# A diffusion backbone step on one core: normalisation moved through the router and pooling products, pooling as banded products, expert results combined by token, modulation chunks spread over the program

## The chip, the cores and the metric

One of the eight cores of a Trainium2 chip runs the whole step, in float32. The metric is the device time of one execution in microseconds (us). PE is TensorE, DVE VectorE, ACT ScalarE, POOL GpSimd, SP SyncE, which only issues transfers here.

## What is computed

128 context tokens and 256 latent tokens of width 1024 go through two layers. Every sublayer reads `rms_norm(x, g) * (1 + scale) + shift`, and its result is added to x times a gate; shift, scale and gate come from a conditioning vector, one for the context and one for the latents. Cut to what matters:

```python
for l in range(2):
    sh1, sc1, g1, sh2, sc2, g2 = split(silu(cond) @ ada_w[l] + ada_b[l])   # ada_w[l]: 1024 x 6144
    h = rms_norm(x, norm_mix_g[l]) * (1 + sc1) + sh1
    m = attention(h) if l == 0 else multi_scale_pool(h, pool_w, pool_scale)
    x = x + g1 * m
    h = rms_norm(x, norm_ffn_g[l]) * (1 + sc2) + sh2
    x = x + g2 * moe(h)        # router h @ (1024 x 36): best of 4 groups, best 2 of its 8 experts
# multi_scale_pool: four groups of 256 features; mean over a centred window of 2, 4, 8, 16 tokens
# minus the token itself, then a 256 x 256 product per group
# moe: 32 experts a layer, each gate and up 1024 x 256 and down 256 x 1024, weighted sum of two
```

## The kernel before

The program is written out engine by engine, with a counting semaphore for each kind of result; the order on each engine is the order of its code. Its stages, one after the other:

- **Opening.** The six vectors of a layer are a product of 1024 x 6144, cut in 12 chunks of 512 columns, numbered 0 to 23 over both layers. A chunk is a load of 2 MB (`load_ada`), eight products on PE (`ada`, L1185), a copy by ACT (`ada_copy`) and four small products that turn the result into columns (`ada_vectors`, L1195). Chunks 0 to 3 are needed before the first product with the attention weights. A load waits for `ada_mm` of the chunk that held its place.
- **QKV products**, nine groups (L1254), with chunks 4 to 11 between them.
- **Attention**, 24 units (16 of the latents with 384 keys, 8 of the context with 128), two heads each. A unit u has its scores on PE (L1297), their maximum on DVE (L913), the exponential on ACT (L670), the reciprocal of the sum on DVE (L920), the scaling by it on POOL (L494, two instructions), transposes on PE (L1325, L1332) and a copy by DVE (L928). In every fourth step PE multiplies with the values (L1314). Chunks 12 to 17 stand in steps 0, 1, 2, 3, 4 and 7. From step 19 on come the output products of the latents (L1360, eight), after the last step those of the context (L1368, eight).
- **Normalisation and router.** `norm_pe`, `norm_act`, `norm_dve` and `modulate_act` form sums of squares by a product with ones (L1375), the root and reciprocal over 128 x 384, and h in feature-major form (hT); the router logits are a product of hT (L1389), turned once more (L1393). `rows_by_token` turns hT into rows by token (L1406), ACT copies them out (L743), and they are written to DRAM; meanwhile `router` on DVE picks the experts. PE counts them (L1415), DVE gives each token its slot in a table of tiles of 64 rows, and POOL gathers the rows.
- **Experts**, 32 tiles a layer and those beyond 64 rows behind them (`extra_tiles`). The weights lie in a ring of four places and a fifth place in `adaw`. SP loads tile s when the tile that held its place has been used: `load_tile` waits for `gu_mm` and `down_mm`. Three transfers make a tile: gate and up 1 MB each, down 1 MB. Results are scattered to DRAM by POOL.
- **Between the layers.** The results are read back (`yrow`) and combined by products with diagonal matrices (L1582); x is normalised, `pool_group` forms window sums on DVE and POOL, and PE multiplies them with the pooling weights (L1599). Then norm, router and experts of layer 1, and the end, where DVE and ACT combine the results by token.

## Time and profile before

| | us |
|---|---|
| runs, median of 3 (lowest to highest) | 945.75 (945.08 to 947.68) |
| the profiled execution, whole | 946.34 |
| its span, first to last instruction | 944.5 |
| PE busy | 759.0 |
| DVE, ACT, POOL busy | 265.7, 188.4, 250.7 |
| moved by the transfers | 294.94 MB, 312 GB/s over the span |
| mean granted clock of TensorE | 0.923 |

Busy time is a mean over stages; what ends last in each stage is read from the chain of waits, the timeline and the windows by stage.

### The profile page before, as it was taken

How to read it: one execution, taken by the hardware profiler on the slowest of the kernel's cores; microseconds unless marked ns; L12 is line 12 of the kernel's file. 1: busy time of each engine (PE TensorE's matmuls, PEld its weight loads, DVE VectorE, ACT ScalarE, POOL GpSimd, SP SyncE). 2: the span in 40 equal slices, each digit the busy share in tenths (PEclk: the TensorE clock that was granted, in tenths of full speed). 3: DMA queues.
4: the chain of work that ended last, by engine and by line, in shares of the span. 5: the costliest groups of instructions: out<-in, count | busy, mean ns of one | idle time of the engine just before them, and what ended most of it. 6: DMA issues, size and time to landing. Idle time of an engine off the chain costs nothing.

```text
span 944.5 us, 12930 instructions
## 1 busy us (share of the span) xinstructions
PE 759.0 (80%) x4601; PEld 408.2 (43%) x4601; DVE 265.7 (28%) x632; ACT 188.4 (20%) x413; POOL 250.7 (27%) x347
## 2 busy tenths in 40 slices
PE   2899989889986999878877867277899978877850
PEld 1534444448833554434433436134555444443420
DVE  0403424532165111111111103976311111111105
ACT  3111144631152011001111102235111101101101
POOL 0000406752002333333232211600243323332212
PEclk9799999989997999999999998677899999999985
DMA  9999779400896999999999959323299999999933
GB/s 325 386 389 370 220 210 387 159 2 1 316 345 234 404 412 411 415 413 413 414 411 413 393 220 396 142 86 133 105 399 407 411 415 416 414 415 413 402 117 155
DMA packets 81126, 294.94 MB, mean 312 GB/s; under 512 B 11624, under 2 KB 12064, under 8 KB 64448
## 3 DMA queue, kind: packets, MB, share of 16 engines
q1 hardware_dynamic: 68064, 273.84, 73.9%
q0 software_dynamic: 11296, 15.09, 4.9%
q10 hardware_dynamic: 1728, 5.51, 1.5%
q8 instruction: 24, 0.39, 0.2%
q14 instruction: 14, 0.11, 0.0%
HBM read 293.84 MB, written 22.02 MB: 334 GB/s over the span
## 4 chain that ended last, share of the span: by engine, by line
PE 50%; DMA 33%; DVE 7%; ACT 3%; issue 3%; SPq 2%; POOL 1%; ACTq 0%; POOLq 0%; DVEq 0%
DMA ring<-in_moe_w_up 25%; PE bank L1492 13%; PE bank L1254 7%; PE bank L1516 6%; PE bank L1185 3%; PE bank L1360 3%; DMA ring<-in_moe_w_down 2%; PE bank L1468 2%; PE bank L1375 2%; PE bank L1195 2%; PE bank L1314 2%; PE bank L1368 2%; PE bank L1389 1%; PE bank L1582 1%; DMA adaw<-in_ada_w 1%
## 5 line engine op out<-in xcount | busy, mean ns | idle before, releaser
L1492 PE MATMUL bank<-ring,qkv 128*64 128x256 f32 x2016 | 247.5, 401 | 64.8 <-DMA ring<-in_moe_w_up 55.6
L1492 PEld LDWEIGHTS bank<-ring,qkv 128*64 128x64 f32 x2016 | 149.4, 144 | 145.2 <-DMA ring<-in_moe_w_up 45.5
L530 POOL DMA_INDIRECT results<-adaw,scur x65 | 66.3, 1020 | 295.5 <-ACT adaw L777 263.2
L1084 DVE COPY qkv<-bank 128x512 f32<-128x512 f32 x64 | 44.2, 691 | 326.5 <-PE bank L1468 298.6
L1516 PE MATMUL bank<-ring,qkv 128*64 128x512 f32 x504 | 122.0, 604 | 1.2 <-DVE qkv L1096 0.8
L520 POOL DMA_INDIRECT adaw<-rows,gcur x65 | 67.9, 1045 | 50.6 <-POOL gcur L517 41.2
L771 ACT ACTIVATE qkv<-bank 128x128 f32<-128x128 f32 x64 | 17.7, 277 | 305.9 <-PE bank L1492 259.6
L1254 PE MATMUL bank<-ring,hT 128*128 128x512 f32 x144 | 65.4, 609 | 1.2 <-DVE hT L855 1.2
L494 POOL TENSOR_SCALAR ring<-ring,rt 128x384 f32<-128x384 f32 (+1 forms) x48 | 49.6, 1047 | 63.2 <-DVE rt L920 63.1
L777 ACT ACTIVATE adaw<-bank 128x512 f32<-128x512 f32 x64 | 38.2, 597 | 140.0 <-PE bank L1516 140.0
L1516 PEld LDWEIGHTS bank<-ring,qkv 128*64 128x64 f32 x504 | 31.0, 136 | 47.5 <-issue 45.6
L1468 PE MATMUL bank<-con,adaw 128*128 128x128 f32 x260 | 43.0, 288 | 6.1 <-DMA adaw<-rows,gcur 5.2
L1254 PEld LDWEIGHTS bank<-ring,hT 128*128 128x128 f32 x144 | 27.3, 194 | 33.9 <-issue 32.6
L1468 PEld LDWEIGHTS bank<-con,adaw 128*128 128x128 f32 x260 | 27.6, 141 | 32.2 <-issue 32.2
L1096 DVE COPY qkv<-bank 128x128 f32<-128x128 f32 x64 | 18.7, 291 | 75.7 <-PE bank L1501 75.7
L1501 PEld LDWEIGHTS bank<-con,qkv 128*128 128x128 f32 x64 | 9.0, 141 | 52.8 <-DVE qkv L1090 49.9
L1185 PE MATMUL bank<-adaw,condT 128*32 128x512 f32 x256 | 30.8, 598 | 1.1 <-DMA adaw<-in_ada_w 1.0
L670 ACT ACTIVATE ring<-bank,ss 128x384 f32<-128x384 f32 (+1 forms) x48 | 24.0, 505 | 37.7 <-DVE ss L913 37.5
L1599 PE MATMUL bank<-hT,xtok 128*128 128x384 f32 x32 | 15.9, 670 | 18.4 <-POOL hT L293 13.3
L1360 PE MATMUL bank<-hT,ring 128*128 128x256 f32 x128 | 29.1, 380 | 0.0
L483 POOL DMA_DIRECT2D ring<-in_cache_k x1 | 0.5, 537 | 105.7 <-PE bank L1254 105.7
L1195 PEld LDWEIGHTS bank<-con,adas 128*128 128x128 f32 x176 | 21.1, 191 | 15.9 <-issue 15.8
(217 smaller groups left out, 783.0 us busy)
## 6 DMA issues: line engine op xcount, KB each, us to landing
ring<-in_moe_w_gate SPq DMA_DIRECT2D x63, 1024.0 KB
ring<-in_moe_w_up SPq DMA_DIRECT2D x63, 1024.0 KB
ring<-in_moe_w_down SPq DMA_DIRECT2D x63, 1024.0 KB
adaw<-in_ada_w SPq DMA_DIRECT2D x16, 2048.0 KB, 12.6
ring<-in_ada_w SPq DMA_DIRECT2D x8, 2048.0 KB, 12.9
ring<-in_attn_w_qkv SPq DMA_DIRECT2D x3, 2048.0 KB, 19.6
adaw<-results SPq DMA_DIRECT2D x12, 512.0 KB, 6.3
ring<-in_attn_w_o SPq DMA_DIRECT2D x1, 4096.0 KB, 19.5
```

The source lines that it names most:

```text
L494: last = G.tensor_scalar(probs[:, u % 4, j, 0:nk], probs[:, u % 4, j, 0:nk], rt[:, 64 + 2 * (u % 4) + j:65 + 2 * (u % 4) + j], None, ALU.mult)
L520: pool.indirect_dma_start(xg[:, b], None, rows, bass.IndirectOffsetOnAxis(ap=gcur[:, b:b + 1], axis=0), bounds_check=row_limit, oob_is_err ...
L530: pool.indirect_dma_start(res, bass.IndirectOffsetOnAxis(ap=scur[:, b:b + 1], axis=0), yout[:, b], None, bounds_check=res_limit, oob_is_er ...
L777: A.activation(yout[:, q], bank[4 + q % 2][:, :], ACT.Copy).then_inc(y_ready, 1)
L1084: V.tensor_copy(xgT[:, p], bank[2][:, :]).then_inc(xgT_ready, 1)
L1185: last = T.matmul(out[32 * j:32 * j + 32, :], condT[:, k, :], ada_place[(i + 2) % 3][:, k, :], start=half == 0, stop=half == 1, skip_group ...
L1195: last = T.matmul(bank[2][:, at:at + 2], adas[:, i % 4, j * P:(j + 1) * P], C("sel2"), start=True, stop=True)
L1254: last = T.matmul(bank[5 + g % 3][:, :], hT[:, k, t * P:(t + 1) * P], wqkv[n][:, k, :], start=k == 0, stop=k == KD - 1)
L1360: last = T.matmul(bank[WO_BANKS[d % 2]][:, 0:NTOK - CTX], wo[:, k, d * P:(d + 1) * P], hT[:, k, CTX:NTOK], start=k == 0, stop=k == KD - 1)
L1468: last = T.transpose(bank[2][:, i * P:(i + 1) * P], xg[:, q, i * P:(i + 1) * P], ident)
L1492: last = T.matmul(bank[p][64 * a:64 * a + 64, 0:2 * P], xk[:, k % 4, k // 4], w[:, :, k, a * P:(a + 1) * P], start=k == 0, stop=k == KD - ...
L1516: last = T.matmul(bank[4 + p][64 * a:64 * a + 64, :], hidT[:, p, 64 * j:64 * j + 64], w[j][:, a * 512:(a + 1) * 512], start=j == 0, stop=j ...
```

## The change

Nothing but the form changes; the same numbers are computed. It has these parts.

1. **Layouts.** The weights of ada_w, QKV, the output product and the experts are laid out ahead of the launch so that each partition reads one run: 16 KB for a chunk (eight runs of 2 KB before), one transfer of 16 KB per partition for gate and up (two of 8 KB before), one of 8 KB for down (two runs of 4 KB before).
2. **Opening.** x and the constants are loaded first; the small vectors go through ACT's queue; chunk 0 stands behind the transposes of x.
3. **Chunks spread.** Chunks 4 to 9 are between the QKV groups, none in attention, 10 to 15 around the router of layer 0, 16 to 21 between the layers, 22 and 23 beside the router of layer 1.
4. **Attention.** The scaling of the probabilities goes from POOL to DVE.
5. **Router.** The logits are products of the plain x (xT) with router weights that were multiplied by the scale (`router_weights`); the sums of squares are products with one column of ones; the reciprocal root enters the logits as one number per token, and the shift's part is added (`logit_shift`). The rows by token are x times the scale, turned, times the root on ACT, and POOL adds a row of the shift (`shift_rows_mm`, `token_rows_mm`).
6. **Between the layers.** The two results of a token are combined by ACT and DVE (`y_first`, `y_both`) and then turned; pooling is a product with scaled weights (L1738), times the root, plus a product of the shift, and then a product with a banded matrix of 128 x 128 with two corners of 8 columns (L1775).

The core of the diff:

```diff
-        AFTER_QKV = {g: 3 + g for g in range(1, 9)}
-        FIRST_SIDE = AFTER_QKV[8] + 1
-        LATE = 2 * NCH - 6
-        SIDE = {step: ("ada", FIRST_SIDE + i) for i, step in enumerate((0, 1, 2, 3, 4, 7))}
+        AFTER_QKV = {g: 3 + g for g in range(1, 7)}
+        LATE = AFTER_QKV[6] + 1
+        BETWEEN = LATE + 6
+        SIDE = {7: ("q", 0), 8: ("q", 1), 11: ("k", 0)}
...
-                for i, w in enumerate((moe_w_gate, moe_w_up)):
-                    sp.dma_start(ring[:, b, i * KD * FE:(i + 1) * KD * FE],
-                                 w[l, bass.ds(e, 1)].rearrange("o (p k) f -> (o p) (k f)", k=KD)).then_inc(arrived, 16)
+                sp.dma_start(ring[:, b, 0:2 * KD * FE],
+                             moe_w_in[l, bass.ds(e, 1)].rearrange("o p n -> (o p) n")).then_inc(arrived, 16)
...
+                if l == 0:
+                    load_ada(BETWEEN)
+                    sp.wait_ge(down_mm, LAST[0] + 1)
+                    load_ada(BETWEEN + 1)
                 sp.wait_ge(x_down[l], 1)
                 n_extra = sp.value_load(extra_e[0:1, EXTRA:EXTRA + 1], min_val=0, max_val=EXTRA)
                 with sp.If(n_extra > 0):
                     load_extra(0)
-                if l == 0:
-                    sp.wait_ge(down_mm, LAST[0] + 1)
-                    load_expert(1, 0)
...
-                for j in range(2):
-                    last = G.tensor_scalar(probs[:, u % 4, j, 0:nk], probs[:, u % 4, j, 0:nk],
-                                           rt[:, 64 + 2 * (u % 4) + j:65 + 2 * (u % 4) + j], None, ALU.mult)
+                    order(V.reciprocal(rt[:, 64 + 2 * (v % 4):66 + 2 * (v % 4)], rt[:, 2 * v:2 * v + 2]))
+                    for j in range(2):
+                        c = 64 + 2 * (v % 4) + j
+                        last = V.tensor_scalar(probs[:, v % 4, j, 0:nk], probs[:, v % 4, j, 0:nk], rt[:, c:c + 1], None,
+                                               ALU.mult)
...
+                for i, t in enumerate(ROW_TILES):
+                    pool.wait_ge(hb_copied, l * 10 + (4, 6, 10)[i])
+                    G.tensor_tensor(xtok[:, t, :], xtok[:, t, :], shift_rows[int(t > 0)], ALU.add).then_inc(rows_ready, 1)
...
+                    pool.wait_ge(shw_mm, 4)
+                    pool.wait_ge(wp_ctx, 1)
+                    by_row = poolw.rearrange("p g k n -> p (g k) n")
+                    G.tensor_tensor(by_row, by_row, mods[:, 1, KD:2 * KD, 1:2].to_broadcast([P, KD, 2 * P]), ALU.mult)\
+                        .then_inc(wp_lat, 1)
...
+            y_both(0)
+            y_both(1)
+            add_experts(0)
+            y_both(2)
+            add_experts(1)
+            pooled_rows(0)
+            add_experts(2)
+            pooled_rows(1)
+            pooled_rows(2)
+            dve.wait_ge(ada_vec, BETWEEN + 6)
+            modulation(1, 2, 5)
...
+                if l == 1:
+                    act.wait_ge(s_rowsout, 48 + 16 * TT)
+                    for n in range(6):
+                        act.wait_ge(x1_mm, n + 1)
```

Where the change moves instructions, first SP's queue at the end of layer 0's experts. Before, the rows from the last load of the tiles on (`L458`, `L451` and `L459` read and test the number of further tiles):

```order
L372 DMA ring<-in_moe_w_down 128x2x1024
L458 TENSOR_LOAD extra_e
L458 ISA x2
L459 COMPARE_AND_BRANCH
L451 TENSOR_LOAD extra_e
L451 ISA x2
L368 ISA
L368 DMA ring<-in_moe_w_gate 128x2048
L368 DMA ring<-in_moe_w_up 128x2048
L372 DMA ring<-in_moe_w_down 128x2x1024
```

and now, from the same place:

```order
L364 DMA ring<-in_moe_w_out 128x2048
L357 DMA adaw<-in_ada_w 128x4096
L357 DMA ring<-in_ada_w 128x4096
L449 TENSOR_LOAD extra_e
L449 ISA x2
L450 COMPARE_AND_BRANCH
L438 TENSOR_LOAD extra_e
L438 ISA x2
L360 ISA
L360 DMA ring<-in_moe_w_in 128x4096
L364 ISA
L364 DMA ring<-in_moe_w_out 128x2048
```

Chunks 16 and 17 stand ahead of the weights of the further tile.

The second place is PE at the router of layer 0. Before, from the logits to the counting of the experts (L1415):

```order
L1389 MATMUL bank<-hT,wr 36x384 x8
L1393 MATMUL bank<-con,rt 128x36 x3
L1195 MATMUL bank<-con,adas 128x2 x4
L1185 MATMUL bank<-adaw,condT 32x512 x8
L1195 MATMUL bank<-con,adas 128x2 x4
L1406 MATMUL bank<-con,hT 128x128 x24
L1415 MATMUL bank<-rt,con 128x32 x6
```

and now, from the last logits (L1450) to the counting (L1533), with the row of the shift (L1500), the rows by token (L1507) and the chunks (L1273, L1283):

```order
L1450 MATMUL bank<-qkv,xT 128x36
L1500 MATMUL bank<-con,mods 128x128 x8
L1507 MATMUL bank<-con,hT 128x128 x16
L1273 MATMUL bank<-ring,condT 32x512 x8
L1500 MATMUL bank<-con,mods 128x128 x8
L1507 MATMUL bank<-con,hT 128x128 x8
L1273 MATMUL bank<-adaw,condT 32x512 x8
L1283 MATMUL bank<-con,adas 128x2 x4
L1533 MATMUL bank<-rt,con 128x32 x6
L1536 MATMUL bank<-con,rt 32x1 x3
L1273 MATMUL bank<-adaw,condT 32x512 x8
L1283 MATMUL bank<-con,adas 128x2 x4
```

Sixteen products of the shift and a second chunk stand ahead of the counting, and a third chunk behind it.

The third is PE between the layers, where one block of products with diagonals (L1582) stood ahead of the norm. Now, with the product of the shift (L1705), the turning of the combined rows (L1716), the sums of squares (L1445), the pooling product (L1738) and a chunk after each:

```order
L1273 MATMUL bank<-adaw,condT 32x512 x8
L1705 MATMUL bank<-xtok,mods 128x256 x16
L1716 MATMUL bank<-con,adaw 128x128 x8
L1273 MATMUL bank<-ring,condT 32x512 x8
L1283 MATMUL bank<-con,adas 128x2 x4
L1716 MATMUL bank<-con,adaw 128x128 x8
L1445 MATMUL bank<-con,qkv 128x1 x8
L1738 MATMUL bank<-hT,xT 128x256 x8
L1273 MATMUL bank<-ring,condT 32x512 x8
L1283 MATMUL bank<-con,adas 128x2 x4
L1716 MATMUL bank<-con,adaw 128x128 x8
```

The two token tiles that follow repeat this, and two more chunks come ahead of the banded products (L1775).

## Rows read from the trace of the kernel before

**Rows 1.** Windows by stage: us, busy time and count by engine, granted clock, transfers.

```profile
44.00:136.50 92.50, 89.96 (x360) 40.22 (x360) 28.65 (x47) 20.05 (x42) 9.86 (x12) 0.98 0.87 296
136.50:207.50 71.00, 61.45 (x384) 30.96 (x384) 33.57 (x68) 35.26 (x110) 42.50 (x36) 0.95 0.57 210
...
241.00:273.40 32.40, 30.04 (x197) 19.03 (x195) 12.37 (x28) 12.25 (x21) 0.00 (x0) 1.00 0.95 367
273.40:304.40 31.00, 22.22 (x163) 13.23 (x162) 18.15 (x81) 11.02 (x14) 4.59 (x6) 0.84 0.70 256
304.40:554.80 250.40, 213.43 (x1440) 109.97 (x1441) 38.55 (x97) 27.97 (x64) 78.80 (x127) 0.96 1.01 405
554.80:643.30 88.50, 54.15 (x221) 31.30 (x222) 50.59 (x93) 21.32 (x38) 21.77 (x16) 0.81 0.44 178
643.30:672.20 28.90, 21.82 (x99) 15.33 (x98) 19.02 (x76) 12.09 (x16) 3.23 (x6) 0.70 0.34 114
672.20:913.70 241.50, 209.46 (x1436) 108.08 (x1436) 37.14 (x95) 27.97 (x64) 74.35 (x123) 0.97 0.94 378
```

**Rows 2.** The page's 40 slices of 23.6 us: transfers in GB/s.

```profile
GB/s 325 386 389 370 220 210 387 159 2 1 316 345 234 404 412 411 415 413 413 414 411 413 393 220 396 142 86 133 105 399 407 411 415 416 414 415 413 402 117 155
```

**Rows 3.** The chain of waits, opening and QKV: start us, us, what.

```profile
16.54 3.23 ACT qkv L611 x6
...
59.82 1.85 PE bank L1185 x16
...
70.60 0.98 PE bank L1195 x8
...
134.64 1.88 PE bank L1195 x16
```

**Rows 4.** The chain of waits in attention and its output products.

```profile
142.20 12.51 DMA adaw<-in_ada_w
...
161.28 2.80 PE bank L1314 x12
...
175.79 2.79 PE bank L1314 x12
...
188.55 2.80 PE bank L1314 x12
...
241.05 14.29 PE bank L1368 x128
```

**Rows 5.** The timeline of DVE and POOL: scaling forms, an attention unit.

```profile
26.19 2.08 DVE L829 TENSOR_SCALAR xtok<-xtok,ss 128x1024 f32<-128x1024 f32 x3 [4.70 <-PE bank L1207]
...
174.60 0.69 DVE L928 COPY ring<-bank 128x512 f32<-128x512 f32 x1 [0.43 <-PE bank L1325]
...
175.67 0.96 DVE L913 TENSOR_REDUCE ss<-bank 128x2 f32<-128x768 f32 x1 [0.38 <-PE bank L1297]
...
181.40 4.90 POOL L494 TENSOR_SCALAR ring<-ring,rt 128x384 f32<-128x384 f32 x4 [2.15 <-DVE rt L920]
```

**Rows 6.** The timeline at the router of layer 0.

```profile
277.77 1.93 ACT L743 ACTIVATE xtok<-bank 128x512 f32<-128x512 f32 x2 [0.85 <-PE bank L1406]
...
282.57 1.42 PE L1415 MATMUL bank<-rt,con 128*128 128x32 f32 x12
```

**Rows 7.** The chain of waits around the end of layer 0's experts.

```profile
535.00 19.69 DMA ring<-in_moe_w_down
...
566.47 4.15 DMA adaw<-results
```

**Rows 8.** The timeline at the end: POOL and DVE, adjacent and at once.

```profile
928.85 1.22 DVE L1160 TENSOR_TENSOR adaw<-adaw,hT 128x1024 f32<-128x1024 f32 x1
...
930.15 3.31 POOL L596 TENSOR_TENSOR xtok<-adaw,xtok 128x1024 f32<-128x1024 f32 x1 [2.42 <-DVE adaw L1160]
931.30 3.25 DVE L1160 TENSOR_TENSOR adaw<-adaw,hT 128x1024 f32<-128x1024 f32 x1
```

**Rows 9.** The chain of waits at the router of layer 1.

```profile
650.53 6.45 DMA rows<-xtok
```

More of the change, by code:

```diff
@@ L1439, in _ @@
                 if l == 0:
-                    for i in range(LATE + 3, 2 * NCH - 1):
+                    for i in range(LATE + 3, BETWEEN - 1):
                         ada(i)
@@ new lines, in _, with feature_sums @@
+                    ada_vectors(BETWEEN + 3)
+                    ada(BETWEEN + 5)
+                    ada_vectors(BETWEEN + 4)
+                    ada_vectors(BETWEEN + 5)
+                    pe.wait_ge(ada_copied, BETWEEN + 6)
+                    def feature_sums(k):
+                        for t in range(TT):
+                            last = stat(2 * KD + 6 + k + 1, 0, sq[:, k % 2, t * P:(t + 1) * P], t, k == 0 and t == 0, k == KD - 1)
+                        last.then_inc(st_mm, 1)
@@ new lines, in _ @@
+                    for n in range(KD):
+                        pe.wait_ge(z_ready, 5 if n < 3 else 6)
+                        if n >= 4:
+                            pe.wait_ge(x_new[2], 2 * (n - 4) + 2)
+                        out, cols = bank[BAND_BANKS[n % 4]], slice(n * P, (n + 1) * P)
+                        parts = ((0, 0, 0, P), (1, P, P, P), (2, 2 * P, 2 * P, P), (1, 2 * P, 3 * P, 8), (2, 2 * P - 8, 3 * P + 8, 8))
+                        for i, (t, a, b, w) in enumerate(parts):
+                            last = T.matmul(out[:, a:a + w], z[:, t, cols], bands[:, n // 2, b:b + w], start=i == 0, stop=True,
+                                            skip_group_check=True)
+                        last.then_inc(mix_mm[2], 1)
+                        if n:
+                            feature_sums(n - 1)
+                        if n == 3:
+                            pe.wait_ge(mods_ready, 4)
+                            logit_shift(1, bank[1])
+                        if n >= 4:
+                            logits(n - 4, range(TT))
```

760 lines of the change are left out of this document (436 added, 324 removed).

## The prediction

> **What bounds it now.** I read the windows by stage first [rows 1]: two expert stages of 250.4 and 241.5 us, and six shorter stages ahead of, between and behind them. In the expert stages the transfers are busy for 1.01 and 0.94 of the time at 405 and 378 GB/s, and the slices of the page stay at 411 to 416 GB/s [rows 2]: the ring of weights sets the pace. It can't run ahead by more than five tiles, so an expert stage begins when the router releases it and lasts as long as its bytes; what comes ahead shifts it one for one. In the other stages the chain of waits runs over PE, with DVE and ACT hops. Two things stand out. In attention the chain waits 12.51 us for a chunk's load [rows 4], while the slices behind it show 159, 2 and 1 GB/s [rows 2]: loads are too late for one place and absent in the next. Between the layers (554.8 to 672.2) transfers are busy for 0.44 and 0.34 of the time and PE for 54.15 of 88.5 us [rows 1]: there is room for chunks, in bytes and partly on PE.
>
> **The change, stage by stage**, against the profiled execution (946.34, span 944.5, 1.8 around it).
>
> *Opening.* ACT's squares of x start at 16.54 [rows 3]. With x (1.57 MB) and the constants (0.59 MB) first, at 386 GB/s [rows 2] they need 5.6 us; with some 4 us for start, landing and the two small steps on the vectors ahead of them the squares start near 9.9, 6.7 earlier. Chunk 0 now stands behind the transposes: 1.85 + 0.98 = 2.83 us [rows 3]. Net -3.9.
>
> *QKV.* Two chunks leave. What leaves the chain is 1.85 after the eighth group, and behind the ninth 1.85 + 1.88 [rows 3], of which I keep 1.9 as the wait for the copies of q and k that these products covered: -3.7.
>
> *Attention.* It lasts 71.0 us from the first scores to the first output product [rows 1]. The wait of 12.51 and six chunks (17.0) leave, but the pace does not follow, since DVE takes over the scaling. A unit costs DVE 0.96 + 0.69 [rows 5], 0.2 for the reciprocal, and now two scalings of 384 elements. Three of 1024 elements take 2.08 [rows 5], 0.69 each; with a fixed part of 0.1 to 0.2 that is 0.3 to 0.4 for 384, taken as 0.35. Together 2.6 us a unit, against 1.2 for one POOL scaling [rows 5], 2.45 a unit. From one value product to the next, four units, it took 188.55 - 175.79 = 12.8 us under POOL [rows 4]; DVE has 10.4 of work in them and waits some 2 us behind the value product: 12.4. So the steady part gains almost nothing. The first six units took 161.28 - 136.5 = 24.8 us [rows 1, 4] with the wait and five chunks; DVE's work there is 6 x 2.6 plus the last norm of q and k and one modulation, 17.2. With 12.9, 12.4, 10.6 and 6.1 for the rest: 59.2, that is -11.8. The bounds are -2 (DVE as slow as POOL was) and -25 (all that leaves counts).
>
> *Latent output products*: untouched. *Context products and logits*: 32.4 before [rows 1]. Now 14.3 [rows 4] plus 64 small products at 0.245 (four in 0.98 [rows 3]), 15.7: 30.0, and 0.3 for the last hop. -2.1.
>
> *Router of layer 0.* DVE picks the experts in some thirty short operations, an estimated 7 us, but PE counts only 282.57 - 273.4 = 9.2 us after them, since the turned rows stand in front and each of the six banks waits for an ACT copy, 1.93 for two [rows 6]. Now ten banks and a chunk stand in front. ACT first copies hT of the context (2.4 us), then five pairs at 2.35 with the gap, and PE adds a second chunk, 2.83: the counting starts 15.2 after the logits, +6.0. The chunk behind the counting takes 2.83, where eight short DVE operations, an estimated 1.5, were waited for: +1.3. POOL's three additions (3.31 or less each, [rows 8]) are done in time for the gather. +7.4 with rounding.
>
> *Experts of layer 0*: 29 tiles, one of them the further one, whose weights were issued at 535.00 and landed 19.69 later [rows 7], right behind tile 31. Two chunks now stand between: 4.19 MB at 425 GB/s, +9.8. The longer runs are worth something: chunks and QKV weights in runs of 2 KB move at 386 to 389, experts in runs of 6 KB on average at 413 to 415 [rows 2]. A fixed 9 ns a run explains both; with 370, the slice behind, 14 ns. A tile has 512 runs before and 256 now, on 16 engines, so it gains 0.14 to 0.22 us; I take 0.2, since the gathers' short rows also slow the experts' slices: -5.8. Net +4.0. The Trainium skill ("DMA: Bandwidth & Descriptors", section "Why small descriptors are slow") speaks against this: it gives a fixed overhead of about 3 cycles a packet beside one per 32 bytes, and at 6 KB that is 1.5%, so that halving the count saves 0.8%, an estimated 0.06 us a tile. The rate of the short runs agrees with more than that.
>
> *Between the layers*, from the arrival of the last weights at 554.8 to the logits, 88.5 before [rows 1]. The results are back 15.8 us after it as before (566.47 + 4.15 [rows 7]). From there PE is the chain: per token tile, eight transposes, eight sums, eight products of 256 columns (1.3 + 2.0 + 3.5) and a chunk 2.83, with ACT's and DVE's combination 1.2 + 1.3 ahead of the first: 39 us from there to the last chunk, waits for ACT and DVE included (some 7); then eight groups of bands, sums and logits at 2.7 and the 16 shift products, 26.5. The logits come 83.8 after the weights: -4.7. POOL's scaling of the pooling weights, 128 x 2048 with two inputs, has twice the elements of the one of 3.31 [rows 8] and falls on the first combination on DVE. DVE's 1.22 became 3.25 beside POOL in [rows 8], so I add 3.0. Net -1.7. The loads fit: 3.1 MB of results, six chunks and five tiles, 31 MB, are 76 us of 120.
>
> *Router of layer 1.* 28.9 before. Ten banks and two chunks bring the counting to an estimated 15.6 after the logits. The x copies of ACT wait for the last write of rows (6.45 [rows 9]), which POOL's addition makes later: 21.8 instead of 13.7 (650.53 + 6.45 - 643.3). +8.1.
>
> *Experts of layer 1*: 27 tiles behind the first five gain 27 x 0.2: -5.4. The end, 30.8, stays.
>
> Sum: -3.9 - 3.7 - 11.8 - 2.1 + 7.4 + 4.0 - 1.7 + 8.1 - 5.4 = -9.1. 946.3 - 9.1 = 937.2; the median lies 0.6 below the profiled execution, so 936.6.
>
> **Rivals.** *A: the released time comes through.* The 12.51 wait and the chunks were the chain in attention, and the rows cost the routers less than I count, because ACT's pairs overlap. It speaks for it that PE is busy for 61 of 71 us there; against it, that POOL's four scalings of 4.90 stand in the chain's place once the chunks are past. -10 more in attention and -6 in the routers: 921. Chance 0.27.
>
> *B: long runs give nothing*, by the rule above or because a run is cut at 8 KB. The rows only show 2 KB against 6 KB. Then +11.2 on the experts: 948, no change. Chance 0.13.
>
> *C, slower: PE's clock between the layers.* The granted clock was 0.81 and 0.70 there [rows 1], after waits of PE for other engines. The new stage holds some 70 us of PE work in short products with hops over ACT and DVE. If a quarter of it runs at 1.2 GHz instead of 2.4, it doubles: +17, so 954. It decides from 6 us on (no gain) and 12 us on (slower). For it speaks that each token tile crosses PE, ACT and DVE three times; against it that the chunks fill PE's waits. Chance 0.17.
>
> Mine has 0.43, with a range of its own of 928 to 946.
>
> **Numbers.** Within 0.3% (942.9 to 948.6) no measurement of this kernel can tell a change. Faster: 0.36 of my 0.43, all of A, 0.02 of B, 0.03 of C, 0.68. Same: 0.06, 0, 0.08, 0.02, 0.16. Slower: 0.01, 0, 0.03, 0.12, 0.16. The range reaches past A's time and nearly to C's, 918 to 951, with about 0.1 left out on either side.
>
> **What would show it.** Squares near 10 and first QKV product near 40; value products of attention 12.4 apart, with DVE, not POOL, in the chain; counting of experts 15 us after the logits in both routers; transfers at 418 or more in full expert slices; the further tile's weights some 255 us after the first tile; DVE's first combination stretched beside POOL. The prediction is wrong where the value products come 10 us apart (A), the slices stay at 413 (B), or the clock falls below 0.8 between the layers (C).

## The result and the profile after

The changed kernel takes 988.81 us, median of 4 runs (983.29 to 989.41), beside 945.41 for the kernel before in the same comparison: a ratio of 1.0443, 95% interval 1.0413 to 1.0474. It is 4.4% slower; 936.6 was predicted, and no rival came near. The profiled execution took 988.32 with a span of 986.5, 42.0 more than before.

The page of the changed kernel, its 40 slices of 24.7 us (compare [rows 2]):

```profile
PEclk9999988998878999999999787757699999999985
...
GB/s 357 427 430 241 193 1 11 1 13 243 176 400 331 421 420 421 420 421 420 422 416 363 144 344 229 326 3 154 298 276 408 419 420 424 421 422 420 415 115 151
```

Most full slices now move 419 to 424 GB/s. The clock falls to 5, 7 and 6 tenths in slices 27 to 29 of the 40, at the end of the stage between the layers and in the router behind it; the transfers show 3 GB/s in slice 27.

The windows by stage answer to [rows 1]. The columns are those of [rows 1]; the stages end at the same events: first scores, first output product, the context's products, logits, first expert product, last weights, logits of layer 1, first expert product, last one.

```profile
42.60:131.10 88.50, 84.20 (x310) 37.57 (x311) 27.94 (x45) 17.70 (x38) 9.87 (x12) 0.98 0.74 274
131.10:189.90 58.80, 46.29 (x239) 23.47 (x240) 45.85 (x105) 32.80 (x105) 0.00 (x0) 0.88 0.02 5
189.90:223.40 33.50, 33.50 (x167) 26.59 (x166) 10.55 (x35) 6.84 (x25) 0.00 (x0) 1.00 0.08 24
223.40:256.90 33.50, 33.50 (x259) 33.50 (x258) 5.38 (x17) 5.03 (x18) 0.00 (x0) 0.85 0.43 173
256.90:299.80 42.90, 37.24 (x242) 21.76 (x241) 21.68 (x80) 18.54 (x28) 12.31 (x10) 0.76 0.82 332
299.80:556.50 256.70, 207.21 (x1442) 113.94 (x1443) 37.88 (x96) 28.00 (x64) 78.43 (x128) 0.97 0.98 403
556.50:670.40 113.90, 103.89 (x548) 83.67 (x549) 27.15 (x63) 23.02 (x43) 9.52 (x11) 0.71 0.49 195
670.40:716.30 45.90, 31.56 (x204) 25.31 (x204) 19.06 (x76) 19.08 (x26) 12.59 (x10) 0.72 0.61 244
716.30:954.00 237.70, 208.01 (x1436) 111.15 (x1436) 37.19 (x95) 28.70 (x65) 74.19 (x123) 0.98 0.93 384
```

Set against the stages before, with the prediction's terms. The window of [rows 1] that ends at 304.40 stops 0.8 us ahead of the first expert product, which came at 305.16; the table counts to the product in both kernels:

| stage | before | after | change | predicted |
|---|---|---|---|---|
| opening, to the first QKV product | 44.2 | 42.6 | -1.5 | -3.9 |
| QKV | 92.4 | 88.5 | -3.9 | -3.7 |
| attention | 71.0 | 58.8 | -12.2 | -11.8 |
| output products of the latents | 33.5 | 33.5 | 0 | 0 |
| context products and logits | 32.4 | 33.5 | +1.1 | -2.1 |
| router of layer 0 | 31.8 | 42.9 | +11.1 | +7.4 |
| experts of layer 0 | 249.7 | 256.6 | +7.0 | +4.0 |
| between the layers | 88.5 | 113.9 | +25.4 | -1.7 |
| router of layer 1 | 28.9 | 45.9 | +17.0 | +8.1 |
| experts of layer 1 | 241.5 | 237.7 | -3.8 | -5.4 |
| end | 30.8 | 32.5 | +1.7 | 0 |

Over half of the 51 us by which the prediction missed lie between the layers, and 9 in the router behind it. Look at PE there: it was busy for 54.15 of 88.5 us before [rows 1] and is busy for 103.89 of 113.9 now, so it hardly waits, and its clock is still at 0.71. Windows of the changed kernel at the places where the clock is low:

```profile
238.00:248.00 10.00, 10.00 (x49) 10.00 (x49) 0.61 (x2) 0.62 (x2) 0.00 (x0) 0.51 0.00 0
276.00:288.00 12.00, 12.00 (x60) 5.99 (x56) 7.01 (x27) 1.19 (x2) 0.00 (x0) 0.50 1.01 425
...
590.00:600.00 10.00, 9.70 (x35) 8.58 (x36) 5.30 (x16) 3.85 (x5) 0.00 (x0) 0.50 0.94 397
...
636.00:670.00 34.00, 34.00 (x162) 34.00 (x161) 3.89 (x11) 5.00 (x12) 3.02 (x5) 0.50 0.15 61
```

In the first and the last PE is busy for the whole window, and so is the loading of its weights (PEld, behind PE in a row, which in the expert stages is some half of PE's). It runs at 1.2 GHz for 34 us without having waited in them. What it does there, PE's groups by line and shape from 649 to 664:

```profile
L1450 PE MATMUL bank<-qkv,xT 128*128 128x36 f32 x23 | 5.7, 407 | 0.0
L1775 PE MATMUL bank<-qkv,adaw 128*128 128x128 f32 x18 | 4.9, 444 | 0.0
L1445 PE MATMUL bank<-con,qkv 128*128 128x1 f32 x20 | 4.8, 352 | 0.0
L1775 PE MATMUL bank<-qkv,adaw 128*128 128x8 f32 x12 | 2.6, 326 | 0.0
```

The new forms: sums of squares of one column (`L1445`), logits of 36 (`L1450`), the bands with their corners of 8 (`L1775`). The kernel before has these steps as products of 384 columns with ones (L1375) and with the logits' weights (L1389). More of the difference is seen in the chain of waits:

```profile
536.19 20.14 DMA ring<-in_moe_w_out
...
556.47 6.67 PE bank L1618 x32
...
576.26 1.15 ACT adaw L731
...
577.44 3.08 DVE adaw L1194
...
684.71 2.36 POOL xtok L492
687.06 0.02 issue
687.08 14.91 DMA rows<-xtok
```

The write of the rows takes 14.91 us instead of 6.45 [rows 9]. The timeline of SP and ACT's queue in the changed kernel shows what was issued around it (L360 and L364 are tiles of weights, L416 the fifth place, L726 the rows):

```profile
679.58 0.33 SPq L360 DMA_DIRECT2D ring<-in_moe_w_in  x1
...
685.21 0.33 SPq L360 DMA_DIRECT2D ring<-in_moe_w_in  x1
...
686.15 0.44 SPq L416 DMA_DIRECT2D adaw<-in_moe_w_in  x1
...
687.08 0.33 ACTq L726 DMA_DIRECT2D rows<-xtok  x1
```

Before 679.58 the transfers stood at 3 GB/s for a slice: the places of tiles 1 and 2 held chunks 22 and 23, which PE takes up only in the router. So these weights are issued right ahead of the rows.

### The profile page after: what moved, and what is told of

Read it like the earlier page. It is cut to its first block, busy times and chain, and to the rows that moved or that the text cites. A ratio compares the mean times of both kernels' runs of the same rounds, so it can differ in the third digit from the quotient of the medians.

```text
span 986.5 us, 13540 instructions
## 1 busy us (share of the span) xinstructions
PE 808.4 (82%) x4981; PEld 491.9 (50%) x4981; DVE 253.3 (26%) x635; ACT 195.1 (20%) x433; POOL 206.5 (21%) x302
## 4 chain that ended last, share of the span: by engine, by line
PE 58%; DMA 28%; DVE 5%; ACT 3%; issue 3%; POOL 1%; SPq 1%; ACTq 0%; POOLq 0%; DVEq 0%
DMA ring<-in_moe_w_in 21%; PE bank L1618 14%; PE bank L1642 7%; PE bank L1342 7%; PE bank L1273 5%; PE bank L1438 3%; PE bank L1594 2%; PE bank L1445 2%; DMA adaw<-rows,gcur 2%; DMA ring<-in_moe_w_out 2%; PE bank L1283 2%; PE bank L1481 2%; PE bank L1450 2%; PE bank L1738 2%; DMA rows<-xtok 2%
## 5 line engine op out<-in xcount | busy, mean ns | idle before, releaser
L1618 PE MATMUL bank<-ring,qkv 128*64 128x256 f32 x2016 | 242.8, 395 | 73.6 <-issue 41.3
L1618 PEld LDWEIGHTS bank<-ring,qkv 128*64 128x64 f32 x2016 | 157.7, 142 | 140.9 <-issue 79.4
L1642 PEld LDWEIGHTS bank<-ring,qkv 128*64 128x64 f32 x504 | 31.0, 136 | 47.5 <-issue 45.6
L492 POOL TENSOR_TENSOR xtok<-xtok,qkv 128x1024 f32<-128x1024 f32 x6 | 14.2, 2372 | 168.0 <-ACT xtok L718 168.0
L1627 PEld LDWEIGHTS bank<-con,qkv 128*128 128x128 f32 x64 | 9.0, 141 | 52.7 <-DVE qkv L1145 51.1
L1283 PEld LDWEIGHTS bank<-con,adas 128*128 128x128 f32 x192 | 24.9, 204 | 20.2 <-issue 19.6
L1273 PE MATMUL bank<-ring,condT 128*32 128x512 f32 x208 | 29.1, 684 | 0.0
L618 ACT ACTIVATE adas<-bank 128x512 f32<-128x512 f32 x24 | 14.3, 596 | 74.3 <-PE bank L1273 74.3
L1283 PE MATMUL bank<-con,adas 128*128 128x2 f32 x192 | 26.5, 262 | 0.6 <-ACT adas L618 0.6
## 6 DMA issues: line engine op xcount, KB each, us to landing
adaw<-in_ada_w SPq DMA_DIRECT2D x11, 2048.0 KB, 12.2
```

What stands on the lines that cost most here:

```text
L1273: last = T.matmul(out[32 * j:32 * j + 32, :], condT[:, k, :], w[:, k, :], start=half == 0, stop=half == 1, skip_group_check=True)
L1283: last = T.matmul(bank[2][:, at:at + 2], adas[:, i % 4, j * P:(j + 1) * P], C("sel2"), start=True, stop=True)
L1618: last = T.matmul(bank[p][64 * a:64 * a + 64, 0:2 * P], xk[:, k % 4, k // 4], w[:, :, k, a * P:(a + 1) * P], start=k == 0, stop=k == KD - ...
L1642: last = T.matmul(bank[4 + p][64 * a:64 * a + 64, :], hidT[:, p, 64 * j:64 * j + 64], w[j][:, a * 512:(a + 1) * 512], start=j == 0, stop=j ...
```

## The experiments

Each is told with its edit, what was on record before it ran, and what it gave. "Before" was measured beside each (medians of 945.1 to 946.3), and the ratios are to it. Times are medians of 4 to 10 runs.

**1. The sums over 128 columns.** The same sums, formed 128 times side by side; column 0 is read.

```diff
-                return T.matmul(bank[b][:, col:col + 1], src, ones[:, 0:1], start=first, stop=last, skip_group_check=True)
+                return T.matmul(bank[b][:, P * col:P * col + P], src, ones, start=first, stop=last, skip_group_check=True)
```

> The changed kernel, with the sums of squares as products with 128 columns of ones instead of one column (only column 0 is read); all else as it was. Theory narrow: PE's granted clock stays at 0.50 from 636 to 675 although PE is busy all the time, because products of one and 36 columns follow each other there; with 128 columns it returns to 1.00, a group of bands, sums and logits goes from 4.7 us to about 2.8, eight of them give -15, and the context products of layer 0 another -2 to -4: 970 to 974. Theory wait: the clock fell because PE waited for DVE at 631 to 632 and it would stay down whatever the columns are; then the wider products only cost more at the low clock, 24 of them at some 0.2 us, +3 to +8: 991 to 996.

Measured: 960.81 (958.0 to 962.05), ratio 1.0156 (1.0126 to 1.0186). More work on PE, and 28.0 us less, well beyond the 15 to 19 that theory narrow had. Its windows for the chunks and pooling products, the bands, and the router of layer 1:

```profile
562.50:622.50 60.00, 51.02 (x317) 36.65 (x316) 19.63 (x47) 15.34 (x26) 5.46 (x5) 0.89 0.78 306
622.50:644.00 21.50, 21.38 (x189) 21.27 (x190) 4.72 (x14) 7.16 (x18) 4.07 (x7) 1.00 0.43 180
644.00:689.50 45.50, 31.37 (x202) 25.12 (x201) 20.95 (x76) 18.97 (x26) 13.24 (x12) 0.74 0.62 248
```

The bands with their sums and logits, 189 records of PE in both kernels, take 21.5 us instead of 38.4 (632.0 to 670.4), at a clock of 1.00. The groups by shape among its bands, from 632 to 640:

```profile
L1445 PE MATMUL bank<-con,qkv 128*128 128x128 f32 x23 | 3.5, 286 | 0.0
L1450 PE MATMUL bank<-qkv,xT 128*128 128x36 f32 x22 | 2.8, 264 | 0.0
L1775 PE MATMUL bank<-qkv,adaw 128*128 128x128 f32 x18 | 2.7, 288 | 0.0
```

A sum of 128 columns takes 286 ns here, one of a single column 352 ns there. A group of bands, sums and logits goes from 4.7 us to 1.09 + 0.77 + 0.59 = 2.45. From the last weights to the logits of layer 1 it is 91.5 us (552.5 to 644.0) instead of 113.9: 16.9 less in the bands and 5.5 less ahead of them, where sums stand too. Another 3.4 us come in layer 0. Both kernels have a wait of PE of 0.81 us for ACT just ahead of the bands, so theory wait falls there.

**2. The logits over 128 columns, the sums left at one.** The products read on behind the 36 columns of the router weights into what follows them, and nobody reads the result of that.

```diff
-                    out = T.matmul(bank[6][:, 16 + 36 * t:52 + 36 * t], xT[:, k, t * P:(t + 1) * P], wrs[:, int(t > 0), k, :],
+                    a = 3392 + (int(t > 0) * KD + k) * (NG + NE)
+                    out = T.matmul(bank[6][:, P * t:P * t + P], xT[:, k, t * P:(t + 1) * P], free[:, a:a + P],
```

> The changed kernel, with the logit products of both routers run over 128 columns instead of 36 (the columns behind the 36 are not read) and the sums of squares left at one column. Theory columns: what holds the clock at 0.50 among the bands is that few columns pass in the time that the weight loads take, whichever product they belong to; 92 more columns in 24 products a layer are some two thirds of what the wide sums added (127 in 24), so the clock rises here too and most of the 28 us come back: 962 to 975. Theory sums: it is the products of a single column that lower it; the logits only begin at the fifth band, so at most the later half gains: 978 to 990.

Measured: 975.06 (972.95 to 984.43), ratio 1.0299 (1.0253 to 1.0344): 14 us less. The windows of this kernel:

```profile
648.00:652.00 4.00, 4.00 (x20) 4.00 (x20) 0.33 (x1) 1.04 (x3) 0.60 (x1) 0.50 0.00 0
...
660.00:664.00 4.00, 4.00 (x29) 3.90 (x29) 0.74 (x2) 1.03 (x3) 0.60 (x1) 0.80 0.00 0
664.00:668.00 4.00, 4.00 (x38) 4.00 (x37) 1.27 (x6) 0.58 (x2) 0.00 (x0) 1.00 0.00 0
```

The clock comes back at about 661, among bands, single-column sums and wide logits. So a single column as such doesn't hold it down; but it comes late, and half of the gain is missing. The traced execution took 984.43, the slowest of the four and only 4 us below the changed kernel's; when the clock came back in the other three (972.95 to 977.06) isn't known. The median is at the far end of theory columns' range, and the traced time lies in the range of theory sums. This run supports theory columns without proving it.

**3. Chunks 22 and 23 among the bands**, so that their places come free for tiles 1 and 2.

```diff
+                        if n == 1:
+                            ada(BETWEEN + 6)
+                        if n == 3:
+                            ada_vectors(BETWEEN + 6)
+                        if n == 5:
+                            pe.wait_ge(wsh_copied, 2)
+                            ada(BETWEEN + 7)
+                        if n == 7:
+                            ada_vectors(BETWEEN + 7)
...
-                ada(BETWEEN + 6 if l else LATE)
+                if l == 0:
+                    ada(LATE)
```

> The changed kernel, with chunks 22 and 23 among the banded products of layer 1 (after the second and the sixth group) instead of inside the router, all else as it was. Theory slots: their weights held two places of the ring until the router, so the transfers were idle from 642 to 680 and the tiles' weights then ran beside the writing of the rows, which took 14.9 us. Now these weights load during the bands, the write takes 5 to 7 us, and the router is 8 to 10 us shorter; as the chunks' 512 columns also lift the clock among the bands, another 4 to 8 come off: 971 to 980. Theory addition: the write was slow and late for another reason (POOL's addition, three writes at once); then it stays at 12 us or more and only what the chunks' place changes is seen: 984 to 990.

Measured: 984.50 (980.96 to 985.71), ratio 1.04 (1.0369 to 1.0431). The chain of this kernel:

```profile
690.74 6.52 DMA rows<-xtok
```

The write takes 6.52 us and the router 37.6 (675.6 to 713.2) instead of 45.9, so theory slots is right on the write. But its time was 971 to 980: the stage between the layers grew by 5 us, since it took in two chunks and its clock stayed at 0.50, and 4 us remain.

**4. Experiment 3 on top of the wide sums**, both diffs at once.

> The changed kernel with sums of 128 columns and with chunks 22 and 23 among the bands, both edits at once. Alone they gave 960.8 and 984.5 against 988.8. Theory slots and clock together: with the clock at 1.00 the two chunks cost 5.7 us among the bands, and the router is shorter by the 8 us of the write (14.75 to 6.5) and by the chunks themselves where they stood on its path (1.9 to 3.8): 954 to 957. If the chunks were hidden in the router and the write is not what its end waits for, 961 to 964.

Measured: 959.14 (957.48 to 961.85), ratio 1.0141 (1.0105 to 1.0177). That is not to be told from wide sums alone, and lies between the two expectations. The write takes 6.06 us for 14.75 and the router is 11.2 us shorter (34.2 for 45.4), but the stage between the layers is 11.4 us longer (102.9 for 91.6): 5.7 for the two chunks, and most of the rest where the clock falls to 0.50, from 632 to about 645, in spite of the wide sums.

**5. The further tile's weights ahead of chunks 16 and 17**, with wide sums.

```diff
-                if l == 0:
-                    load_ada(BETWEEN)
-                    sp.wait_ge(down_mm, LAST[0] + 1)
-                    load_ada(BETWEEN + 1)
                 sp.wait_ge(x_down[l], 1)
                 n_extra = sp.value_load(extra_e[0:1, EXTRA:EXTRA + 1], min_val=0, max_val=EXTRA)
                 with sp.If(n_extra > 0):
                     load_extra(0)
+                if l == 0:
+                    load_ada(BETWEEN)
+                    sp.wait_ge(down_mm, LAST[0] + 1)
+                    load_ada(BETWEEN + 1)
```

> The changed kernel with sums of 128 columns, and the loads of chunks 16 and 17 behind the weights of the further tile on SP's queue instead of ahead of them. The prediction's term: the two chunks' 4.19 MB delay that tile by 9.8 us; behind it they load while its results are on their way: 960.8 - 9.8, so 950 to 953. If chunk 16 then comes too late for PE, half is lost: 954 to 957. If the further tile waits for something else, 960 to 962.

Measured: 947.49 (945.04 to 950.68), ratio 1.0026 (1.0006 to 1.0045), 13.3 less, below the expected range. In the chain of this kernel, the last transfer and the further tile's first product:

```profile
523.48 19.43 DMA ring<-in_moe_w_out
...
543.04 5.28 PE bank L1618 x32
```

The expert stage is 245.6 us (297.5 to 543.0) instead of 256.0 with wide sums alone, 10.4 less, against the 9.8 of the term; where the other 3 us come from isn't settled. Chunk 16 starts at 551.9 right behind the tile, so it isn't late.

**6. Wide sums, chunks among the bands, further tile first**, the diffs of 1, 3 and 5.

> The changed kernel with all three edits: sums of 128 columns, chunks 22 and 23 among the bands, further tile's weights ahead of chunks 16 and 17. If the gains add, 944 to 948, which is no worse than the kernel before; if the router of layer 1 and the further tile share a cause, 950 or more.

Measured: 949.03 (947.77 to 952.19), ratio 1.0038 (1.0020 to 1.0057). The gains don't add: the chunks among the bands again bring nothing.

**7. Experiment 5 without POOL's additions** (three in each router). It leaves out the shift in the rows that the experts read.

```diff
-                for i, t in enumerate(ROW_TILES):
-                    pool.wait_ge(hb_copied, l * 10 + (4, 6, 10)[i])
-                    G.tensor_tensor(xtok[:, t, :], xtok[:, t, :], shift_rows[int(t > 0)], ALU.add).then_inc(rows_ready, 1)
```

> The kernel of wide_tile_first without POOL's three additions of the shift to the rows by token, in both routers; ACT starts the writing of a tile of rows as soon as it has copied it. It leaves out the shift in the rows that the experts read, so its outputs differ from the reference; all else is as it was. Theory addition: the third write in router 1 starts at 647.7 instead of some 645.3 because of the addition, and the loads of tiles 1, 2 and the fifth place (issued at 640 to 647) are ahead of it; the write would start 2.4 us earlier and land 3 to 6 us earlier: 941 to 945. Theory queue: the write takes its 14.8 us because of the loads ahead of it and the addition only adds its own 2.4 us: 944.5 to 946.

Measured: 948.41 (944.2 to 951.84), ratio 1.003 (1.0008 to 1.0052), no difference to experiment 5. The chain:

```profile
644.43 17.80 DMA rows<-xtok
```

In experiment 5 it is issued at 647.72 and takes 14.79 us. The whole kernel is 1.8 us earlier at this point, the loads beside the write too; counted from the logits (630.86 for 632.70) the write is issued 1.5 us earlier and lands 1.6 us later, 31.4 for 29.8 us behind them. So the addition isn't what makes it late. Why it then takes 3 us longer isn't settled.

**8. The table of the gathers ahead of the turning of x** in the router of layer 1, on top of experiment 5. Both stand in PE's order; the turning waits for ACT, and ACT for the write of the rows.

```diff
-                if l == 1:
-
-                    pe.wait_ge(hb_copied, 20)
-                    for n in range(6):
...
                 last.then_inc(tab_mm, 1)
...
                 if l == 1:
 
+                    pe.wait_ge(hb_copied, 20)
+                    for n in range(6):
```

> The kernel of wide_tile_first with the turning of x back to rows (for the end of the program), in the router of layer 1, behind the product that makes the table of the gathers instead of ahead of it. ACT's copies of x wait for the last write of rows (14.8 us), and on PE the table waits behind them. If that chain is what the router's end waits for, the gathers start as soon as the rows are written, at 663 instead of 673, with x turned meanwhile; of these 10 us some 4 to 6 remain, since PE still has the 5.8 us of the gates and the 3.8 of x in front of the first expert: 941 to 944. If the end waits for the write alone, 947 as before.

Measured: 942.91 (940.74 to 945.35), ratio 0.9972 (0.9946 to 0.9997): 4.6 less. With three edits the changed form is a little under the kernel before. The first expert product is 128.8 us behind the further tile's (542.2 to 671.0) instead of 135.8.

**9. The same with chunks 22 and 23 among the bands**, the diffs of 1, 3, 5 and 8.

> The kernel of x_after_table with chunks 22 and 23 among the bands as well: the write is then 6.0 instead of 14.8 us, and the bands are 6 us longer. Together with the earlier table: 940 to 944, no more than 2 us from x_after_table. If it gains 5 us or more against it, the write was what held the router.

Measured: 950.68 (949.07 to 953.35), ratio 1.0056 (1.0035 to 1.0077), 7.8 more than experiment 8; neither of the two expectations. Its windows among the bands:

```profile
619.00:632.00 13.00, 13.00 (x60) 9.80 (x60) 1.48 (x4) 2.20 (x6) 1.20 (x2) 0.50 0.43 183
632.00:642.00 10.00, 10.00 (x90) 10.00 (x90) 1.69 (x6) 2.46 (x6) 1.21 (x2) 0.99 0.95 365
```

The logits are 11.8 us later than in experiment 8 (641.97 for 630.17, where DVE takes them): 5.7 for the two chunks and 6 for the clock, which falls again from 619 to 632 although the sums are wide. PE had no wait there; ahead of the fall stand 32 records of the logits' shift with 36 columns and the first of a chunk's products with 2. The router behind is 3.7 shorter.

**10. Experiment 9 with wide logits too**, the diffs of 9 and 2.

> The kernel of x_chunks (950.7, with the clock at 0.50 from 619 to 632 among the bands in spite of the wide sums) with the logits over 128 columns too. Theory columns: the shift's products of 36 columns and the logits lowered it; with wide logits the clock stays at 1.00 behind the first logits and some 3 to 5 us come back: 945 to 948. If the waits of PE for DVE and ACT at 605 to 608 lowered it, or the place of the chunks did, no change or 1 us slower: 950 to 952.

Measured: 946.85 (943.2 to 950.9), ratio 1.0017 (0.9994 to 1.0040), 3.8 less. Among the bands the clock is at 0.50 from 620 to about 627 only. Again more columns gave time back.

**11. The layouts alone, on the kernel before.** One run of 16 KB per partition for a chunk and for gate and up, 8 KB for down.

```diff
-                for i, w in enumerate((moe_w_gate, moe_w_up)):
-                    sp.dma_start(ring[:, b, i * KD * FE:(i + 1) * KD * FE],
-                                 w[l, bass.ds(e, 1)].rearrange("o (p k) f -> (o p) (k f)", k=KD)).then_inc(arrived, 16)
+                sp.dma_start(ring[:, b, 0:2 * KD * FE],
+                             moe_w_in[l, bass.ds(e, 1)].rearrange("o p n -> (o p) n")).then_inc(arrived, 16)
```

> The kernel before, with the layouts alone (one run per partition for chunks, QKV weights, output product, gate and up, down). The prediction's term: 0.2 us a tile over 56 tiles, -11, and 2 to 4 us in the opening: 931 to 935, with full slices at 418 to 422 GB/s. The rival that long runs give nothing: 943 to 947. If the long transfers make the small ones (gathers, writing of rows) wait longer, the router stages lengthen by some us each and the gain is smaller: 936 to 942.

Measured: 937.52 (936.25 to 939.17), ratio 0.9911 (0.9887 to 0.9935). The page of this kernel:

```profile
GB/s 347 427 350 354 242 187 424 133 2 1 326 347 222 388 418 421 421 421 420 421 419 414 388 229 387 151 91 134 105 383 406 421 423 423 420 425 420 408 114 154
```

414 became 421 GB/s. At 3.15 MB a tile that is 0.13 us, not 0.2. From the first expert product of layer 0 to the further tile's it is 247.4 us (304.0 to 551.4) instead of 249.7, 0.08 a tile; the expert stage of layer 1 is 3.5 us shorter, 0.13 a tile, and 1.2 come in front. Rival B falls. The time is in the range of the third expectation, but not for its reason: the routers did not get longer.

**12. The scaling on DVE alone, on the kernel before.**

```diff
-                    V.reciprocal(rt[:, 64 + 2 * (v % 4):66 + 2 * (v % 4)], rt[:, 2 * v:2 * v + 2]).then_inc(sc_recip, 1)
+                    order(V.reciprocal(rt[:, 64 + 2 * (v % 4):66 + 2 * (v % 4)], rt[:, 2 * v:2 * v + 2]))
+                    for j in range(2):
+                        c = 64 + 2 * (v % 4) + j
+                        last = V.tensor_scalar(probs[:, v % 4, j, 0:nk], probs[:, v % 4, j, 0:nk], rt[:, c:c + 1], None,
+                                               ALU.mult)
+                    last.then_inc(sc_normed, 1)
```

> The kernel before, with the scaling of the probabilities on DVE instead of POOL and nothing else. The prediction's reasoning: DVE with 10.4 us in four units keeps a pace of 12.4 against POOL's 12.8, and the wait for chunk 12 stays, so -1 to -3: 943 to 945. If DVE's work is worse placed beside the chunks' products (it copies and takes maxima too), +2 to +6: 947 to 951.

Measured: 946.16 (941.99 to 947.51), ratio 0.9999 (0.9983 to 1.0015), no difference, between the two expectations. The value products in the chain of this kernel:

```profile
161.21 2.79 PE bank L1311 x12
175.72 2.79 PE bank L1311 x12
188.13 2.79 PE bank L1311 x12
```

The last two are 12.4 us apart, the pace that the prediction worked out. The output products start 4.9 us earlier (202.5), and the whole gains nothing: the first expert product comes 2.5 us earlier, and from there the two kernels differ by no more than their runs do.

**13. Layouts, DVE and the change's opening, on the kernel before.** The vectors go to ACT's queue, x is loaded first, chunk 0 stands behind the transposes.

```diff
-            load_ada(0)
-            sp.dma_start(con[:, :], consts).then_inc(s_const, 16)
...
+            sp.dma_start(xtok[:, 0, :], x_prompt[0]).then_inc(s_x, 16)
+            sp.dma_start(con[:, :], consts).then_inc(s_const, 16)
+            for i in range(4):
+                load_ada(i)
...
-            ada(0)
             pe.wait_ge(s_x, 32)
...
-            for i in range(1, 4):
+            for i in range(4):
                 ada(i)
-                ada_vectors(i - 1)
+                if i:
+                    ada_vectors(i - 1)
```

> The kernel before with the layouts (alone 937.5), the scaling on DVE (alone no difference) and the change's opening (x and constants first, vectors on ACT's queue, chunk 0 behind the transposes). In the changed kernel the first QKV product came 1.5 us earlier than before (42.6 for 44.2). If that is the opening's doing, 934.5 to 936.5; by the prediction's term of -3.9, 932 to 934; if with the chunk's wait gone (the long runs bring chunk 12 in time) DVE's pace counts as well, another 1 to 2 less.

Measured: 941.29 (940.3 to 947.67), ratio 0.9963 (0.9938 to 0.9988), slower than the layouts alone and outside what was expected. Its chain:

```profile
29.95 1.90 PE bank L1178 x16
31.87 8.76 DMA ring<-in_ada_w
...
48.53 2.04 PE bank L1247 x2
```

The squares start at 13.60, but the first QKV product only at 48.53. Chunk 0 holds its place until 31.9, and chunk 3 needs that place. The changed kernel issues five chunks by 5.54 and doesn't pay for this.

**14. The same, with chunk 0 ahead of the transposes**, as in the kernel before:

```diff
+            ada(0)
             pe.wait_ge(s_x, 32)
```

> The kernel before with the layouts, the scaling on DVE, and x and the constants loaded first with the vectors on ACT's queue, but chunk 0 ahead of the transposes as before. before_open lost 4.7 us at the first QKV product (48.5 for 43.8), since chunk 3 waits for the place that chunk 0 holds. If that is so, the squares start at 13.3 and the first QKV product comes at 41 to 42.5: 932 to 936, the fastest of all. If the vectors on ACT's queue are what was late, it stays at 938 to 941.

Measured: 933.17 (929.81 to 935.96), ratio 0.9869 (0.9819 to 0.9919). The first QKV product comes at 40.95. It is the fastest kernel of the study, 1.3% under the one before. It has parts 1 and 4 of the change and part 2 without the move of chunk 0; places for chunks, norms, pooling and combination are those of the kernel before. How the 4 us below experiment 11 divide between the opening and DVE isn't separated.

**15. The table ahead of x in that kernel**, the move of experiment 8 made in it.

> The kernel of before_best (933.2) with the turning of x behind the table of the gathers in the router of layer 1, as in x_after_table, where it gave 4.6 us. Here the write of the rows takes 6.5 instead of 14.8 us, so the table waits less: 930 to 932. If the table is not what the end of this router waits for, 933.

Measured: 935.57 (934.51 to 938.29), ratio 0.9895 (0.9853 to 0.9938), no gain, where 930 to 933 was expected. In the changed kernel the table stood behind a write of 14.8 us; here no write takes more than 6.8, which is the likely reason.

## Why the prediction was wrong, step by step

**Attention and QKV were right in sum**: -12.2 and -3.9 for -11.8 and -3.7. In the changed kernel the value products in the chain of waits are

```profile
163.64 2.79 PE bank L1399 x12
175.42 2.79 PE bank L1399 x12
```

11.8 apart where 12.4 was worked out. From the first scores on, the parts of the stage are 19.6, 12.9, 11.8, 10.3 and 4.2 us for 17.2, 12.9, 12.4, 10.6 and 6.1, so that the sum comes out so well is in part luck. Releasing 29.5 us of PE and waits gave 12: DVE's steps fill most of the chain between the value products, 2.55 us of DVE a unit where 2.6 was worked out. Rival A, which let 10 us more come through, was wrong here.

**The step that failed is "eight groups of bands, sums and logits at 2.7"**, and with it the 39 us of pooling products. They were costed from durations at a clock of 1.00, and the clock went to rival C at a price of 17 us, which supposed that a quarter of PE's work would be slow because PE waits for ACT and DVE. Of the 27.1 us missed between the layers, 14.9 are in the bands with the shift's products (41.4 us for 26.5) and 8.2 in the part with the pooling products and its first combination (52.7 for 44.5, the 3.0 of contention counted in). In the other 4.0 the combination starts later, 19.8 us behind the last weights for 15.8, as the further tile's products took 6.67 us instead of 3.69 and ACT copies the products of the shift first.

The place was right and the cause was not, as far as the bands go. There PE did not wait: in 34.00 us of 34.00 it was busy, at 0.50. In the stretch at 0.50 it ran products of 1, 8 and 36 columns among some of 128. In three kernels columns were added with no work taken away (experiments 1, 2 and 10), and 28.0, 14 and 3.8 us came back; in experiment 1 the bands run at 1.00 with the same wait ahead of them. The rival had "against it that the chunks fill PE's waits"; what counted was what the products between them look like. Two things stay open. In experiments 4 and 9 the clock fell in the bands although the sums were wide, so wide sums alone don't keep it up. And earlier in the stage the rival's own cause may have had a share: the clock is at 0.50 at 580.5 and again at 590.3, right behind waits of PE of 4.83 and 3.04 us, in the changed kernel and at the same places in experiment 1.

The Trainium skill ("TensorE: Matmul & The Clock Gate", section "What's actually happening") says that the clock is set by how busy PE has been recently. If busy is read as the profile's busy share, the clock should have been 1.00 in the bands and not 0.50; here the measurement decides, and the busy share of PE is no sign of a high clock.

With wide sums, 27.1 of the miss between the layers shrinks to 4.7 (91.5 us for the 86.8 that the prediction has with its 3.0 of contention). The contention was there, but smaller: DVE's first combination took 3.08 us beside POOL's scaling and 1.28 the next time, 1.8 more and not 3.0.

**The router of layer 1**: +17.0 for +8.1. The prediction carried over the write's 6.45 us and made it later; it took 14.91. The loads fit "76 us of 120" by their sum, but not by their places: two places of the ring held chunks that PE uses only in the router. Experiment 3 shows it: 6.52 us once the places are free, landing 21.7 us behind the logits, where the prediction had 21.8. Experiment 7 shows that POOL's addition isn't the cause. Moving the chunks did not pay, since it took as much among the bands as it gave in the router (11.4 for 11.2 us in experiment 4), or more (11.8 for 3.7 in experiment 9); changing PE's order by one block did (experiment 8).

**The router of layer 0 and the context**: +11.1 and +1.1 for +7.4 and -2.1. The counting of the experts comes 16.3 us behind the logits, 15.2 was worked out. From the counting to the first expert product it is 26.6 us, 4.0 more than before, where 1.3 was worked out. The chunks behind the counting run at 0.50 from 276 to 288 and take up to 3.64 us instead of 1.85. That this is the cause isn't shown: in experiment 1 two of them take 1.92 each, and it is 26.9 us there. In the context's stage the count of 64 small products was right; it includes the sixteen of the logits' shift (L1458), which took 4.1 us for 3.9. But the clock falls while these sixteen run and is at 0.51 from 238 to 248, and the two groups that follow take 6.0 and 4.6 us instead of 3.1.

**Experts**: +7.0 and -3.8 for +4.0 and -5.4. The two chunks cost 10.4 for 9.8 (experiment 5). The long runs give 0.08 us a tile in layer 0 and 0.13 in layer 1 for 0.2 (experiment 11), which accounts for both misses to within 1.1 us. The fixed cost of a run was in the prediction twice, as 9 ns from the full slices and as 14 ns from a slice at 370 GB/s, and it took 0.2, nearer to the upper one. 9 ns gives 0.14, and that is what the chunks' slices show as well: 386 to 389 GB/s became 427 to 430 with runs of 16 KB instead of 2 KB, some 9 ns a run. The estimate from the Trainium skill ("DMA: Bandwidth & Descriptors", section "Why small descriptors are slow") was 0.06 a tile; the measured values lie between it and the prediction's.

**The opening**: -1.5 for -3.9. The squares start at 13.3 and not at 9.9. The prediction counted the bytes of x and constants and two small steps on the vectors, but not the loading of the vectors, which are six issues on ACT's queue. The last of them is issued at 3.15 and lands 8.71 us later, beside the loads of the chunks. The 1.7 us more at the end were not followed up.

What the experiments took off, one on top of the other, from 988.8: wide sums -28.0, the further tile first -13.3, the table first -4.6. That is 942.9, 6 us above the forecast.

## What to carry to other kernels

Before you replace a few wide products by many narrow ones on PE, cost them at 1.2 GHz as well. Where such a stretch is on the path, try widening the moving side of the narrow ones: at a clock of 1.00 eight sums took 1.95 us with 128 columns and 1.84 with one, and where the clock came back it gave far more than that. Don't take PE's busy time as a sign of its clock: the weight loads were busy as long as PE both in the changed kernel's bands at 0.50 (34.00 us) and in those of experiment 1 at 1.00 (21.27 of 21.50). And where a load is moved, check whose place it holds and until when; the sum of the bytes doesn't show that, the issue times on SP's queue do.

## What was unexpected of the hardware

A product of 128 columns was faster than one of a single column in the same place, 286 ns at a clock of 1.00 for 352 at 0.50; the kernel as a whole became 28 us faster by doing more.

DVE's short steps stop while POOL adds. The timeline of experiment 9, in the router of layer 1:

```profile
646.93 4.69 POOL L492 TENSOR_TENSOR xtok<-xtok,qkv 128x1024 f32<-128x1024 f32 x2 [9.58 <-ACT xtok L718]
646.95 2.46 DVE L1062 SCALAR_TENSOR_TENSOR rt<-rt 128x96 f32<-128x96 f32 x1
649.44 0.25 DVE L1029 TENSOR_REDUCE rt<-rt 128x3 f32<-128x96 f32 x1
649.73 2.01 DVE L1030 TENSOR_TENSOR rt<-rt 128x96 f32<-128x96 f32 x1
```

Steps of 0.26 us took 2.46 and 2.01, each until one of POOL's additions was over. It is 4 us of DVE in each router. In experiment 7, where the additions are gone, these steps take their short time, but the counting comes 15.5 us behind the logits of layer 1 as in experiment 5: DVE's 4 us were not on the path there.
